# Two layers and two directions of a gated linear attention: the decay's log-sigmoid computed at full width with exp(-ln u) in place of a reciprocal, spread over more places

## What is computed

```python
la_f = split_heads(jax.nn.log_sigmoid((ga_f @ gate_w[0] + gate_b[0]).astype(F32)) / GLA_TAU, GLA_HEADS)
la_b = split_heads(jax.nn.log_sigmoid((ga_b @ gate_w[1] + gate_b[1]).astype(F32)) / GLA_TAU, GLA_HEADS)
o = gla_direction(q, k, v, la_f) + flip_t(gla_direction(flip_t(q), flip_t(k), flip_t(v), flip_t(la_b)))
...
def gla_direction(q, k, v, log_a):
    ...
    cum = jnp.cumsum(log_a.astype(F32).reshape(b, h, n, c, dk), axis=3)
    ...
    scores = jnp.einsum('bhnik,bhnjk,bhnijk->bhnij', q, k, pair.astype(q.dtype))
    intra = jnp.einsum('bhnij,bhnjv->bhniv', scores, v)
```

## Time and profile before

| | |
|---|---|
| median of 3 runs | 3534.58 us (3534.37 to 3536.81) |
| the profiled execution, its own time | 3536.15 us |
| its span in the profile | 3534.0 us |
| PE busy | 3423.2 us (97%) |
| DVE busy | 2287.7 us (65%) |
| ACT busy | 1852.8 us (52%) |
| DMA queue of the weights | 557.94 MB |

### The profile page before, as it was taken

One profiled execution on the slowest core, in us unless ns is written; L12 is line 12 of the kernel. 1 busy time (PEld: TensorE's weight loads), 2 busy tenths in 40 slices (PEclk: granted clock), 3 DMA queues, 4 the chain that ended last, 5 costly groups with the idle time before them and its releaser, 6 DMA issues.

```text
span 3534.0 us, 41526 instructions
## 1 busy us (share of the span) xinstructions
PE 3423.2 (97%) x16098; PEld 2768.5 (78%) x16098; DVE 2287.7 (65%) x3066; ACT 1852.8 (52%) x2528; POOL 165.0 (5%) x243
## 2 busy tenths in 40 slices
PE   8989999989999999999999999999999999999998
PEld 6877678778687877788888888878777888888886
DVE  5877565885666566566666666765665566666665
ACT  4564655646554356554554544543665555445544
POOL 3033000051000000000000000000000000000000
PEclk9999999999999999999999999999999999999999
DMA  7544355544364355456556556553554665565564
GB/s 204 161 128 130 108 173 169 157 129 135 102 196 149 104 157 142 152 184 189 185 179 197 182 187 193 179 158 106 159 141 152 196 191 185 181 195 185 179 198 153
DMA packets 399891, 578.50 MB, mean 164 GB/s; under 512 B 25505, under 2 KB 222617, under 8 KB 399312
## 3 DMA queue, kind: packets, MB, share of 16 engines
q1 hardware_dynamic: 393344, 557.94, 51.5%
q0 software_dynamic: 5904, 16.75, 1.6%
q10 hardware_dynamic: 448, 1.18, 0.1%
HBM read 570.78 MB, written 4.98 MB: 163 GB/s over the span
## 4 chain that ended last, share of the span: by engine, by line
PE 82%; DVE 9%; ACT 5%; issue 2%; DMA 2%; ACTq 0%; DVEq 0%
PE PS L711 79%; DVE WL L1873 3%; PE PS L708 3%; ACT WH L1326 2%; DMA RAW<-in_w_in 1%; DVE AR L2007 1%; DVE ZA L2059 1%; ACT ZA L1396 0%; ACT L1597 0%; DVE AR L2340 0%; ACT AR L1681 0%; ACT L1636 0%; DVE AR L2271 0%; DVE SM L2273 0%; ACT AR L1688 0%
## 5 line engine op out<-in xcount | busy, mean ns | idle before, releaser
L1873 DVE TENSOR_TENSOR WL<-RAW,WH 128x1024 fp32r<-128x1024 f32 x1056 | 1294.0, 1230 | 954.5 <-ACT WH L1326 951.8
L1326 ACT ACTIVATE WH<-RAW 128x1024 fp32r<-128x1024 f32 x1056 | 1106.5, 1056 | 1049.8 <-PE PS L711 666.7
L711 PE MATMUL PS<-WH,Ah 128*128 128x512 f32 x3520 | 1423.7, 404 | 25.6 <-DVE WL L1873 13.0
L711 PE MATMUL PS<-WL,Ah 128*128 128x512 f32 x3520 | 1381.5, 392 | 0.0
L711 PE MATMUL PS<-WH,Al 128*128 128x512 f32 x3520 | 1380.2, 392 | 0.0
L711 PEld LDWEIGHTS PS<-WH,Ah 128*128 128x128 f32 x3520 | 666.8, 189 | 194.7 <-issue 32.3
L711 PEld LDWEIGHTS PS<-WL,Ah 128*128 128x128 f32 x3520 | 665.9, 189 | 143.8
L711 PEld LDWEIGHTS PS<-WH,Al 128*128 128x128 f32 x3520 | 667.3, 190 | 136.8 <-issue 6.7
L711 PE MATMUL PS<-WH,Zh 128*128 128x512 f32 x704 | 278.3, 395 | 0.6
L711 PE MATMUL PS<-WL,Zh 128*128 128x512 f32 x704 | 274.2, 389 | 0.0
L711 PE MATMUL PS<-WH,Zl 128*128 128x512 f32 x704 | 274.2, 389 | 0.0
(11 more groups left out here) (320 smaller groups left out, 2151.6 us busy)
## 6 DMA issues: line engine op xcount, KB each, us to landing
RAW<-in_w_in SPq DMA_DIRECT2D x368, 512.0 KB, 3.7
RAW<-in_w_up SPq DMA_DIRECT2D x704, 256.0 KB, 3.1
RAW<-in_w_down SPq DMA_DIRECT2D x176, 512.0 KB, 3.9
RAW<-in_w_out SPq DMA_DIRECT2D x64, 512.0 KB, 3.6
RAW<-in_w_o SPq DMA_DIRECT2D x64, 512.0 KB, 3.7
RAW<-in_w_in SPq DMA_DIRECT2D x64, 256.0 KB, 3.0
AR<-in_c POOLq DMA_DIRECT2D x2, 1600.0 KB, 8.0
...
```

The costliest lines, as they stand in the source:

```text
L711: return T.matmul(o, lhs, rhs, start=start, stop=stop, skip_group_check=True)
L1326: act(WH[:, j % NW, 0:n], raw_view(j), ACT.Copy).then_inc(*w_hi())
L1873: tt(WL[:, j % NW, 0:w], raw_view(j), WH[:, j % NW, 0:w].bitcast(F32), SUB).then_inc(*w_lo())
```

## The change

It does five things in `gla(l)`, in both layers; the rest of the kernel is as it was.

- Both directions are computed in one instruction of 128x1024 instead of two of 128x512: `za`, `ze`, `zl` on ACT and `zu`, `zc`, `zd`, `zn`, `zm`, `zp`, `zs`, `la` on DVE.
- `zr`, the reciprocal on DVE, is gone. ACT takes exp(-ln u) in its place (`zi`).
- ACT takes |z| straight from PSUM; `zn` on DVE comes later.
- The steps are spread: `za` and `ze` in Z+1, `zu` to `zd` in Z+2, `zl` in Z+3, `zn` and `zi` in Z+4, `zm` in Z+5, `zp` in Z+6, `zs` and `la` in Z+7. PE's diagonal scores are in Z+8 and now wait for `la` and `za`. The levels start two places later.
- In the levels DVE goes through direction 1 before direction 0, so that `pa` of direction 1 stands before `qk` of direction 0.

```diff
@@ -460,16 +460,14 @@
...
-                if k == 0 and 1 <= n < 9:
-                    lev_dve += [f"pa{d}{n - 1}"]
...
-                    lev_dve += [f"qk{d}{n}"] if k == 1 else []
-        ga_ = ["le", "za0", "ze0", "za1", "ze1", "zl0", "zl1"] + lev_act
-        gd = ["l0", "l1", "l2", "l3", "l4", "l5", "one", "gatc", "zn0", "zn1"]
-        gd += [f"{n}{d}" for d in R2 for n in ("zu", "zc", "zd")]
-        gd += [f"{n}{d}" for d in R2 for n in ("zr", "zm", "zp", "zs", "la")] + ["at0", "at"] + lev_dve
+            for d in (1, 0):
+                n, k = divmod(i - d, 3)
+                lev_dve += [f"pa{d}{n - 1}"] if k == 0 and 1 <= n < 9 else [f"qk{d}{n}"] if k == 1 and 0 <= n < 8 else []
+        ga_ = ["le", "za", "ze", "zl", "zi"] + lev_act
+        gd = ["l0", "l1", "l2", "l3", "l4", "l5", "one", "gatc", "zu", "zc", "zd", "zn", "zm", "zp", "zs", "la", "at0", "at"] + lev_dve
...
@@ -612,7 +610,7 @@
-        SPZ = [[ar(6144 + 1024 * k + 512 * d, 512) for k in R4] for d in R2]
+        SPZ = [ar(6144 + 1024 * k, 1024) for k in R4]
@@ -1141,8 +1139,7 @@
                     ins.then_inc(*g_pe(m(f"z{d}")))
-                yield
-                for _ in range(5):
+                for _ in range(8):
                     yield
                 yield from e.until("gqk")
@@ -1156,7 +1153,8 @@
 
-                T.wait_ge(*g_dve.at(m("zn1")))
+                T.wait_ge(*g_act.at(m("za")))
+                T.wait_ge(*g_dve.at(m("la")))
                 T.wait_ge(*s_act.at(f"{l}.gqk.k"))
                 scores(GQ, GK, ((0, 0), (1, 1)), ("dgx", "dg", 4))
@@ -1700,18 +1698,20 @@
                 yield from e.until("ga")
                 yield
                 yield
-                for d in R2:
-                    z, x, _, _ = SPZ[d]
-                    A.wait_ge(*g_dve.at(m(f"zn{d}")))
-                    act(x, z, ACT.Abs).then_inc(*g_act(m(f"za{d}")))
-                    A.wait_ge(*g_act.at(m(f"za{d}")))
-                    act(x, x, ACT.Exp, scale=-1.0).then_inc(*g_act(m(f"ze{d}")))
-                yield
-                for d in R2:
-                    _, x, u, _ = SPZ[d]
-                    A.wait_ge(*g_dve.at(m(f"zd{d}")))
-                    act(x, u, ACT.Ln).then_inc(*g_act(m(f"zl{d}")))
-                for _ in range(5):
+                yield
+                z, x, u, _ = SPZ
+                A.wait_ge(*g_pe.at(m("z1")))
+                act(x, PS[:, 5:7, :].rearrange("p b n -> p (b n)"), ACT.Abs).then_inc(*g_act(m("za")))
+                A.wait_ge(*g_act.at(m("za")))
+                act(x, x, ACT.Exp, scale=-1.0).then_inc(*g_act(m("ze")))
+                yield
+                yield
+                A.wait_ge(*g_dve.at(m("zd")))
+                act(x, u, ACT.Ln).then_inc(*g_act(m("zl")))
+                yield
+                A.wait_ge(*g_act.at(m("zl")))
+                act(u, x, ACT.Exp, scale=-1.0).then_inc(*g_act(m("zi")))
+                for _ in range(4):
                     yield
                 yield from e.until("gqk")
                 yield
@@ -2320,37 +2320,34 @@
                 cp(flat(GAT[0:16, :, :]), PS[0:16, 4, :]).then_inc(*g_dve(m("gatc")))
                 yield
                 yield
-                for d in R2:
-                    V.wait_ge(*g_pe.at(m(f"z{d}")))
-                    ts(SPZ[d][0], bank(5 + d), -1.0, None, MUL).then_inc(*g_dve(m(f"zn{d}")))
-                yield
-                for d in R2:
-                    z, x, u, c = SPZ[d]
-                    V.wait_ge(*g_act.at(m(f"ze{d}")))
-                    ts(u, x, 1.0, None, ADD).then_inc(*g_dve(m(f"zu{d}")))
-                    V.wait_ge(*g_dve.at(m(f"zu{d}")))
-                    ts(c, u, -1.0, None, ADD).then_inc(*g_dve(m(f"zc{d}")))
-                    V.wait_ge(*g_dve.at(m(f"zc{d}")))
-                    tt(c, x, c, SUB).then_inc(*g_dve(m(f"zd{d}")))
-                yield
-                for d in R2:
-                    z, x, u, c = SPZ[d]
-                    la = LA[:, d, :, :].rearrange("p t n -> p (t n)")
-                    V.wait_ge(*g_act.at(m(f"zl{d}")))
-                    rcp(u, u).then_inc(*g_dve(m(f"zr{d}")))
-                    V.wait_ge(*g_dve.at(m(f"zr{d}")))
-                    tt(c, c, u, MUL).then_inc(*g_dve(m(f"zm{d}")))
-                    V.wait_ge(*g_dve.at(m(f"zm{d}")))
-                    tt(c, c, x, ADD).then_inc(*g_dve(m(f"zp{d}")))
-                    V.wait_ge(*g_dve.at(m(f"zp{d}")))
-                    stt(la, z, 0.0, c, MAX, ADD).then_inc(*g_dve(m(f"zs{d}")))
-                    V.wait_ge(*g_dve.at(m(f"zs{d}")))
-                    ts(la, la, -1.0 / 16, None, MUL).then_inc(*g_dve(m(f"la{d}")))
-                    yield
-                yield
+                yield
+                z, x, u, c = SPZ
+                la = LA.rearrange("p d t n -> p (d t n)")
+                yield
+                V.wait_ge(*g_act.at(m("ze")))
+                ts(u, x, 1.0, None, ADD).then_inc(*g_dve(m("zu")))
+                V.wait_ge(*g_dve.at(m("zu")))
+                ts(c, u, -1.0, None, ADD).then_inc(*g_dve(m("zc")))
+                V.wait_ge(*g_dve.at(m("zc")))
+                tt(c, x, c, SUB).then_inc(*g_dve(m("zd")))
+                yield
+                yield
+                V.wait_ge(*g_act.at(m("za")))
+                ts(z, PS[:, 5:7, :].rearrange("p b n -> p (b n)"), -1.0, None, MUL).then_inc(*g_dve(m("zn")))
+                yield
+                V.wait_ge(*g_act.at(m("zi")))
+                tt(c, c, u, MUL).then_inc(*g_dve(m("zm")))
+                yield
+                V.wait_ge(*g_dve.at(m("zm")))
+                tt(c, c, x, ADD).then_inc(*g_dve(m("zp")))
+                yield
+                V.wait_ge(*g_dve.at(m("zp")))
+                stt(la, z, 0.0, c, MAX, ADD).then_inc(*g_dve(m("zs")))
+                V.wait_ge(*g_dve.at(m("zs")))
+                ts(la, la, -1.0 / 16, None, MUL).then_inc(*g_dve(m("la")))
                 yield
                 yield from e.until("gqk")
-                V.wait_ge(*g_dve.at(m("la1")))
+                V.wait_ge(*g_dve.at(m("la")))
                 V.wait_ge(*g_pe.at(m("dg")))
                 blocks = bass.AP(tensor=AT.tensor, offset=AT.offset, ap=[AT.ap[0], [512, 4], [384, 2], [1, 128]])
                 for t in R2:
```

## The result

The changed kernel takes 3504.16 us (median of 4 runs, 3502.82 to 3506.6), the kernel before 3534.47 us in the same comparison; the ratio is 0.9914, with an interval of 0.9902 to 0.9927. The change saves 30 us, 0.9%. The sign was right, and so was the place of the gain, PE's stops in the gla mixer; one of these stops was read wrongly, and the gain was put too low. A second comparison of the same kernel gave 3504.96 us against 3534.21, 0.9917 [0.9904, 0.9931], a saving of 29.3 us.

What follows compares the result with a forecast made beforehand. PE, busy 97% of the span, was taken as the bound; its gla waits of 19.0 us plus 8.35 of slow clock, less 1.0 for a new wait, gave 26.35 saved: 3508.3 us, own range 3505.5 to 3511, wider range 3504.5 to 3516.

Steps and rivals of the forecast that it cites:

- The stop at Z+6: First layer: PE stops 2.88 us at Z+6, said to wait for the decay's last scaling (L2348); the change ends it.
- Idle: Gates to output products: PE's waits of 19.0 us over both layers go, less 1.0 us for a new wait.
- The new wait for `la`: At Z+8 PE waits for the decay's last step, 0 to 1.2 us, taken as 0.5 a layer, 1.0 us lost.
- The cost of a stop beyond its wait: Behind PE's stops in the mixer, matmuls partly at 1.2 GHz: 8.35 us over both layers, to be gained.
- Behind the levels: Output products to first transposes of `diff`: 40.37 us a layer, paced by an ACT and DVE chain; taken as 0 change.
- The levels: Masked copy's 4.35 us wait at i = 13 goes through the reorder; the shift alone would move it to i = 19.
- The reciprocals: On DVE, 3.35 us each, two a layer, 13.4 us in all; with four steps behind, they delay splits and stop PE.
- The longer stop on ACT: Rival, 12%: exp of Z+4 ends 1.4 us later, PE waits 1.9 us a layer at Z+8, slow clock follows: 3514.3 us.
- the levels' wait stays: Rival, 6%: the masked copy waits at i = 19 for something else held up by ACT's chunk; 12.7 us stay, 3521.0 us.
- the weights bound Z+5: Rival, 5%: weight loading bounds PE at Z+5; only the levels' 12.7 us gained, 3521.9 us, or nothing, about 3534.6.
- The slower case: Rival, 2%: direction 0's scaling in the levels is late in all 16 places, at 2.5 us each: 3548 us.
- The marks: Expected later profile: no Z+5 weight wait, 0 to 1.2 us at Z+8, no 4.35 us copy wait, stretch near 144 us.

Runs made afterwards that it cites:

- packed: Kernel before with the levels' reorder and exp(-ln u) on ACT for the reciprocal, half-width, decay steps and first scores in their old places: 3520.02 us, ratio 0.996.
- packed_late: `packed` with only the first scores and the levels two places later, at Z+8 and Z+9: 3510.66 us, ratio 0.9926.
- dg_late: `zi_early` with the first scores and the levels one more place later, at Z+9 and Z+10: 3503.77 us, ratio 0.9915.
- zi_early: Changed kernel with ACT's exp of -ln u one place earlier, right behind the logarithm at Z+3: 3505.01 us, ratio 0.9919.
- rcp_spread: Changed kernel with the reciprocal back on DVE as two halves, at Z+3 and Z+4, instead of ACT's exp: 3511.96 us, ratio 0.994.
- dg_early: Changed kernel with the first scores and the levels one place earlier, at Z+7 and Z+8, decay steps unmoved: 3519.83 us, ratio 0.9963.
- decay: Changed kernel without the reorder: in the levels the scaling of direction 0 again stands ahead of the masked copy: 3521.37 us, ratio 0.9962.
- qk_thrice: Changed kernel with the scaling of direction 0 in the levels done three times instead of once: 3509.09 us, ratio 0.9929.
- reorder: Kernel before with only the levels' masked copy of direction 1 put ahead of the scaling of direction 0: 3519.6 us, ratio 0.9962.

## Why the prediction missed, and what of it was right

**In short.** The forecast was too high for two reasons, and one wait was read wrongly. First, what the stops cost beyond their waits was put at 8.35 us and was 9.7, and behind the levels 0.7 us were gained where I had 0. Second, what scatters ahead of z1, about 2 us of the measured saving, was put at nothing, in the sum and in the range; with a term for it the range would have held the time. The wait read wrongly is that at Z+6: it was put down to the decay's last scaling, and PE waited there for ACT's copy of k. It changed neither the sum nor the sign.

**The bound** was right: the gain came from idle PE in one stretch a layer and from the clock behind it, and ACT's DMA wait of 6.05 us was no bound of its own. Waits of this kind still exist after the change, 2.35 and 1.49 us at Z+8 and Z+9, where the splits are far enough ahead.

**The stop at Z+6: read wrongly.** The prediction took it from the view's releaser in the first layer, L2348. But in the kernel before PE's scores wait for `zn1` and for the copy of k (L1481), and not for `la`. In the second layer PE goes on at 2353.21, while the scaling still runs until 2353.24; the copy of k ended at 2353.06 (kernel before: timelines of ACT, DVE and PE).

```profile
2352.47 0.59 ACT L1481 ACTIVATE AR<-PS 128x512 f32<-128x512 f32 x1
```

```profile
2352.81 0.43 DVE L2348 TENSOR_SCALAR AR<-AR 128x512 f32<-128x512 f32 x1
```

```profile
2353.21 1.68 PE L711 MATMUL PS<-AR 64*128 64x128 f32 x16 [1.50 <-ACT AR L1481]
```

In the first layer the copy ends at 1116.53 and PE goes on 0.14 us later, at 1116.67; here it is 0.15. The copy stands on ACT behind the split that had found its tile missing for 6.05 us. So the path ran from DVE's late splits over the loading and ACT's stream to PE. That is why `packed`, whose last scaling ends at 1109.10, stops until 1112.56 all the same, and why later scores end this stop in `packed_late`. That the stop went as forecast was partly luck: the prediction gave no account of ACT's copy, and without the two places for the scores it could have stayed, as in `packed`.

**Idle.** Forecast 19.0 less 1.0 = 18.0 us; measured 10.18 + 8.93 less twice 0.69 = 17.7.

**The new wait for `la`.** Forecast 0.5 us a layer; it is 0.6 (0.69 of idle less the 0.1 that is there without it). The chain held to 0.05 us, counted from z1: the exp ends at 16.8 us (worked out 16.8), `zs` at 23.45 (23.49), `la` done at 25.39 (25.39). The additions, which had no row at this width, took 0.69 us, and I had taken 0.7. (The 0.69 for a half-width step is not in the earlier trace rows; the trace of the kernel before has it, for `zm` and `zp`.)

**The cost of a stop beyond its wait: the mis-sized term.** I had 8.35 us, from slow clock alone. The busy time of the same matmuls fell by 147.80 - 142.64 = 5.16 and 147.15 - 142.61 = 4.54, so 9.70. My pairs of windows in the earlier trace rows gave 4.62 and 3.73 for the two layers, so 0.54 and 0.81 were missing. This is not slow clock: in windows of 1 us the granted clock in the two stretches of the kernel before is under 0.99 only inside my windows and in the idle time next to them. It is the edges of the stops. The last matmul ahead of one counts 0.39 us, where in the flow the next starts 0.23 us after it, so a stop takes 0.16 more than its wait, three times a layer. And the tile of 2.99 us that I took as normal stood between two stops itself; `dg_late` against `zi_early` shows 2.73 for a tile in the flow. I estimate both from these rows at some 0.5 us a layer; the rest of the second layer's 0.81 I have not placed. What a stop costs beyond its idle is better read from the whole stretch against one without stops. With `zi_early`'s 148.2 us as the stretch without a stop, the added busy time is 1.7 us for a stop of 2.0 (`packed_late`), 1.5 for 2.6 (`rcp_spread`), 2.7 for 3.3 (`dg_early`), 2.6 for 4.35 (`decay`), but 0.3 for 1.16 (`qk_thrice`) and nothing for 0.6.

**Behind the levels.** Forecast 0; measured 0.7 us gained over both layers (28.1 from z1 in the profiled executions, less 27.4 in the stretches). The stretch after the output products is 0.55 us longer, with eight more matmuls in it, and what follows is shorter by more. That it is paced by a chain is borne out by the clock: in the kernel after PE was busy for 37.01 us at 1.00 in the first layer and for 38.59 at 0.96 in the second, and both took 40.92. That this part keeps its length was right for shifts of two and three places and would have been wrong for one: `dg_early` lost 1.9 us a layer there. "Paced by a chain, so it stays" was luck in part; where the chunks fall against the chain decides it.

**The levels.** The wait moved to i = 19 with the shift and ended with the order: shown by `decay` and `reorder`. Room for the scaling at i = 19: forecast 0.6 to 1.6 us, measured 1.3.

**The reciprocals.** I wrote that the reciprocal fills a place on DVE and that this makes PE stop. For the split at Z+5 of the kernel before that fits; but with the reciprocals gone and the decay's other steps left in place (`packed`) PE stopped for as long (4.9 us of idle a layer against 5.9 and 4.3 in `reorder`), now for ACT. The 13 to 15 us of this half belong to exp, spreading and later scores together.

**The sum.** 17.7 + 9.7 + 0.7 = 28.1 us, against 26.35. That makes 3506.5 of the 3534.58 that I started from. The other 2 us are scatter ahead of z1, for which my range had no term at all: its low end, 3505.5 for the forecast's own cases, carried `la` and one slow stretch only. The span shows the same: forecast 3507.7 us, measured 3501.2, and 4.7 of the 6.5 between them lie ahead of z1. How much of such scatter four runs catch is chance: the kernel before alone gave medians from 3533.03 to 3536.12 us in the comparisons of these runs.

**The rivals.** The longer stop on ACT (12%) did not come: the exp starts 0.01 us behind its table load, so the drain that the Trainium skill counts ("ScalarE: Activation LUTs", "What ACT_TABLE_LOAD costs") does not appear here. One load for ln and exp, as the Trainium skill has it in the same page's "Table sets: the hidden batching unit", doesn't either: `zi_early` has a load of 1.28 us between the two. That the levels' wait stays (6%) is what happens in `decay`, and the reorder prevented it. That the weights bound Z+5 (5%) is out, since the stops went with no change to the loading. The slower case (2%) is out by `qk_thrice`.

**The marks.** All hold but one: I wrote 144 us for the stretch from gates to output products and had forgotten that the products themselves move two tiles; 148.8 less 5.5 is 143.3.
